# The third modulation vector's row sum behind the values' product, `v`'s weight split ahead of that vector's parts, and the fifth vector's last parts amid later work

## What is computed

```python
mod = (silu(c) @ ada_w + ada_b).reshape(bsz, 6, dm)          # six vectors of 1024: ada 0 to 5
shift_a, scale_a, gate_a, shift_f, scale_f, gate_f = mod     # ada 2 is gate_a, 3 is shift_f, 4 is scale_f
h = rms_norm(x, norm1_g) * (1.0 + scale_a) + shift_a
proj = h @ w_in                                              # columns u, v, o, i, f, p
y_m = mlstm_group(u, v, o, i, f, ...)                        # convolution, q, k, decayed scores, their sum with v
y_p = pool_group(p, w_pool, b_pool, pool_scale)
x = x + gate_a * (concat([y_m, y_p]) @ w_out)
h = rms_norm(x, norm2_g) * (1.0 + scale_f) + shift_f         # then routing and 32 experts, then the second block
```

## Time and profile before

| | |
|---|---|
| median of 3 runs | 2020.95 us (2019.82, 2020.95, 2025.08) |
| the profiled execution's own time | 2019.93 us |
| its span | 2018.2 us |
| busy: TensorE, VectorE, ScalarE, GpSimd | 1944.6, 1184.1, 965.7, 186.4 us |
| mean granted TensorE clock | 0.992 |

### The profile page before, as it was taken

One profiled execution on the slowest core, in us unless ns is written; L12 is line 12 of the kernel. 1 busy time (PEld: TensorE's weight loads), 2 busy tenths in 40 slices (PEclk: granted clock), 3 DMA queues, 4 the chain that ended last, 5 costly groups with the idle time before them and its releaser, 6 DMA issues.

```text
span 2018.2 us, 22881 instructions
## 1 busy us (share of the span) xinstructions
PE 1944.6 (96%) x8920; PEld 1562.1 (77%) x8920; DVE 1184.1 (59%) x1548; ACT 965.7 (48%) x1469; POOL 186.4 (9%) x250
## 2 busy tenths in 40 slices
PE   4989989999999999999999999999999999999998
PEld 3757758888878888758888888887777778888886
DVE  7766699998989999763543323325345453333323
ACT  3443258888878888744232223224455542222221
POOL 3110111122111110020000000000021100000000
PEclk8999999999999999999999999999999999999999
DMA  8465379999999999951322232222212133323201
GB/s 292 146 214 193 125 248 370 366 377 378 380 363 357 362 373 366 345 169 69 105 84 89 99 105 84 94 94 68 86 59 83 43 115 105 103 85 105 94 32 42
DMA packets 199976, 366.49 MB, mean 182 GB/s; under 512 B 13466, under 2 KB 83879, under 8 KB 199866
## 3 DMA queue, kind: packets, MB, share of 16 engines
q1 hardware_dynamic: 180960, 342.91, 48.4%
q10 hardware_dynamic: 8858, 11.46, 1.7%
q0 software_dynamic: 10048, 10.62, 1.5%
HBM read 365.05 MB, written 24.65 MB: 193 GB/s over the span
## 4 chain that ended last, share of the span: by engine, by line
PE 81%; DVE 7%; DMA 6%; ACT 3%; issue 2%; SPq 1%; POOL 0%; DVEq 0%; POOLq 0%; ACTq 0%
PE ps L263 79%; DMA raw<-in_w_expert_gate 4%; DVE wlo L210 3%; DMA raw<-in_w_in 1%; ACT whi L191 1%; PE ps L2012 1%; PE ps L2039 1%; SPq L919 1%; DMA raw<-in_ada_w 0%; ACT YB L2104 0%; PE ps L2667 0%; DVE XT1l L2095 0%; DVE XT0l L2095 0%; DVE acc L260 0%; ACT XN L703 0%
## 5 line engine op out<-in xcount | busy, mean ns | idle before, releaser
L210 DVE TENSOR_TENSOR wlo<-raw,whi 128x1024 fp32r<-128x1024 f32 (+1 forms) x576 | 674.1, 1215 | 296.7 <-ACT whi L191 294.4
L191 ACT ACTIVATE whi<-raw 128x1024 fp32r<-128x1024 f32 (+1 forms) x576 | 573.5, 1048 | 233.4 <-PE ps L263 196.4
L263 PE MATMUL ps<-hT5h,whi 128*128 128x512 f32 x352 | 137.0, 389 | 0.6 <-DVE hT5l L260 0.6
L263 PE MATMUL ps<-hT3h,whi 128*128 128x512 f32 x352 | 137.0, 389 | 0.6 <-DVE hT3l L260 0.6
L263 PE MATMUL ps<-hT3h,wlo 128*128 128x512 f32 x352 | 137.0, 389 | 0.0
L263 PE MATMUL ps<-hT3l,whi 128*128 128x512 f32 x352 | 137.0, 389 | 0.0
L263 PE MATMUL ps<-hT5h,wlo 128*128 128x512 f32 x352 | 137.0, 389 | 0.0
L263 PE MATMUL ps<-hT5l,whi 128*128 128x512 f32 x352 | 136.9, 389 | 0.0
L2530 DVE TENSOR_TENSOR tmpT<-tmpT,ps 128x512 f32<-128x512 f32 x44 | 30.1, 684 | 139.7 <-PE ps L263 139.7
L263 PE MATMUL ps<-whi,XT1h 128*128 128x512 f32 x256 | 102.8, 401 | 1.5 <-DVE XT1l L2095 1.5
L263 PE MATMUL ps<-whi,XT0h 128*128 128x512 f32 x256 | 102.9, 402 | 1.2 <-DVE XT0l L2095 1.1
(11 more groups left out here) (446 smaller groups left out, 4045.0 us busy)
## 6 DMA issues: line engine op xcount, KB each, us to landing
raw<-in_w_expert_gate SPq DMA_DIRECT2D x64, 1024.0 KB, 7.4
raw<-in_w_expert_up SPq DMA_DIRECT2D x64, 1024.0 KB, 8.1
raw<-in_w_expert_down SPq DMA_DIRECT2D x64, 1024.0 KB, 7.0
raw<-in_ffn_w_gu SPq DMA_DIRECT2D x44, 1024.0 KB, 5.1
raw<-in_ffn_w_down SPq DMA_DIRECT2D x20, 1024.0 KB, 5.0
raw<-in_ada_w SPq DMA_DIRECT2D x24, 512.0 KB, 5.4
raw<-in_w_in SPq DMA_DIRECT2D x8, 1024.0 KB, 6.0
raw<-in_a_w_in SPq DMA_DIRECT2D x8, 1024.0 KB, 10.7
```

Source lines behind the costliest of these rows:

```text
L191: e.activation(hi[:, c], raw[:, c], ACT.Copy).then_inc(self.S("w_hi"), 1)
L210: e.tensor_tensor(lo[:, c], raw[:, c], hi[:, c].bitcast(F32), ALU.subtract).then_inc(self.S("w_lo"), 1)
L263: return e.matmul(o, l, r, start=start, stop=stop, skip_group_check=True)
```

## The change

The same instructions are issued on every engine; their order differs.

- TensorE: `ada_row_pe(3)` stands behind `n_pe("v")` instead of ahead of it.
- ScalarE: `ada_row_act(3)` stands behind the copies of the values and the split of the pooling group instead of ahead of `skip`.
- VectorE: `W.low` of `v`'s first item ahead of parts 12 to 15, that of its second right behind them; then `pool_out(2)` and `(3)`, parts 16 and 17, `W.low` of `wo`'s first item, parts 18 and 19. Parts 20 to 23 move between `scaled`, `finish`, `W.low` and `mix_low`.
- SyncE: `wo`'s first two items are loaded ahead of parts 16 and 18 instead of 18 and 22.

```diff
@@ first_sync
-                W.load(e, {2: 6, 4: 7, 8: 8, 18: 9, 22: 10}.get(m, 0))
+                W.load(e, {2: 6, 4: 7, 8: 8, 16: 9, 18: 10}.get(m, 0))
@@ first_pe
             pool_pe(e, 3)
+            n_pe(e, W.index["v"], "v", hT1, 0, KC, None)
             ada_row_pe(e, 3)
-            n_pe(e, W.index["v"], "v", hT1, 0, KC, None)
             sums_pe(e, 0)
@@ first_act
             W.high(e, W.index["v"][1] + 1)
-            ada_row_act(e, 3)
             for h in range(4):
                 skip(h)
...
                 e.activation(hT1[0][:, 4 + gi, :], PT[:, gi, 16:528], ACT.Copy).then_inc(S("mix_hi"), 1)
+            ada_row_act(e, 3)
             W.high(e, W.index["wo"][1] + 1)
@@ first_vec
             pooled(3)
-            ada_parts(e, own, 12, 13)
-            ada_parts(e, own, 14, 15)
             W.low(e, W.index["v"][0] + 1)
-            ada_parts(e, own, 16, 17)
+            ada_parts(e, own, 12, 13, 14, 15)
+            W.low(e, W.index["v"][1] + 1)
             pool_out(2)
             pool_out(3)
+            ada_parts(e, own, 16, 17)
+            W.low(e, W.index["wo"][0] + 1)
             ada_parts(e, own, 18, 19)
-            W.low(e, W.index["v"][1] + 1)
-            ada_parts(e, own, 20, 21)
-            W.low(e, W.index["wo"][0] + 1)
-            ada_parts(e, own, 22, 23)
...
             scaled(1)
+            ada_parts(e, own, 20)
             finish(0)
             W.low(e, W.index["wo"][1] + 1)
+            ada_parts(e, own, 21)
             scaled(2)
             finish(1)
             mix_low(0, UC[0], 5)
+            ada_parts(e, own, 22)
             scaled(3)
             mix_low(1, UC[1], 6)
             finish(2)
             mix_low(2, UC[2], 7)
+            ada_parts(e, own, 23)
             finish(3)
```

## The result

The changed kernel takes 2011.18 us (median of 6 runs, 2008.71 to 2012.20), the kernel before 2020.38 (6 runs, 2017.86 to 2025.08): a ratio of 0.9957 [0.9948, 0.9967], 0.43% or about 9 us faster. The profiled execution took 2008.71 us with a span of 2007.0, 2.5 us under the median. The page reads like that of before: the chain is TensorE's still, 84% of it (before 81%).

What follows compares the result with a forecast made beforehand. TensorE bounds the kernel; its 6.08 us wait for VectorE's chain of loads is charged again through half clock. 2019.93 - 9.4 + 0.6 = 2011.1, set at 2011.5 us; range 2008 to 2018.

Steps and rivals of the forecast that it cites:

- the sum: Whole kernel: profiled 2019.93 us, less 9.4 gained by TensorE, plus 0.6 lost on VectorE, gives 2011.1 us.
- `n_pe("v")` first, then the row sum: TensorE after `pool_pe`: `v` product starts without a wait, row sum at full clock, `sums_pe(0)` 9.38 us earlier.
- the copy's wait: TensorE ahead of `sums_pe(0)`: waiting for the copy of `v`'s last bank, 1.08 us, would be covered by the row sum.
- The second half of `v`'s weight: VectorE's split `W.low(v1)` would be ready before TensorE asks at 156.66; cost nothing.
- the cover: Time by which `v`'s second split is ready before TensorE asks: 1.8 us; without it each microsecond of delay costs one.
- `ada_row_act(3)`: ScalarE: its two copies, behind those of `v` and `mix_hi`, end near 171.8 and cost nothing, with 0.5 us margin.
- Parts 20 to 23: VectorE amid `scaled` and `finish`: cost 0.6 us, TensorE's wait for `mix_low(1)` growing from 0.7 to 1.3 us.
- SyncE: `wo2`'s load goes out later, about 188.4, lands at 195.4 and is in time with a cover of 4.5 us.
- The rest shifts as a whole: Behind 217 every wait hangs on TensorE or VectorE, so everything later moves earlier together.
- The rival that nothing arrives at the end: Expert stage: if its start is set by something not moved, the gain is lost there; 2020 us, chance 0.10.
- The scatter: Times of whole runs: half of the 5 us between the runs before was allowed for in the range.

Runs made afterwards that it cites:

- Experiment 1: Kernel before with only TensorE's and ScalarE's moves, VectorE's and SyncE's order left as it was: 2018.96 us against 2019.95, ratio 0.9999.
- experiment 5: Changed kernel with ScalarE's `ada_row_act(3)` back at its old place ahead of `skip`: 2019.97 us against 2019.86 for the kernel before, ratio 0.9999.
- experiment 2: Kernel before with six matmuls of no use filling TensorE's wait ahead of the row sum: 2018.04 us against 2019.95, ratio 0.9992.
- Experiment 3: Changed kernel with the split of `v`'s second item behind `pool_out` and parts 16 and 17: 2017.53 us against 2019.95 for the kernel before.
- Experiment 8: Changed kernel with parts 20 and 21 and `mix_low(1)` earlier on VectorE: 2009.75 us against 2019.78 for the kernel before, ratio 0.9955.
- Experiment 6: Changed kernel with `wo0` and `wo1` loaded at their old places: 2017.04 us against 2019.86 for the kernel before, ratio 0.9986.
- experiment 4: Changed kernel with parts 20 to 23 right behind 18 and 19: 2020.19 us against 2019.95 for the kernel before, ratio 1.0004.
- second trace: The changed kernel run once more, unaltered: 2011.10 us against 2019.78 for the kernel before, ratio 0.9960.
- seventh: Changed kernel with three matmuls of no use in TensorE's pause ahead of the ranking: 2008.98 us against 2019.86 for the kernel before, ratio 0.9950.
- ninth: Changed kernel with parts 20, 21 and `mix_low(1)` earlier on VectorE, fillings ahead of ranking and first gathered rows: 2009.18 us, again 2008.47 us.

## Why the prediction was right

The forecast was 2011.5 us and 2011.18 was measured, by the mechanism of the sum: the marks show a gain of 9.10 us where the sum had 8.8. That the median came within 0.3 us of the forecast is in part luck. The interval of the ratio leaves a gain of 6.7 to 10.5 us, and the forecast took only about half of the 1.0 us between the profiled execution and the median, without saying why; the whole of it would have given 2012.1. By its steps:

- **`n_pe("v")` first, then the row sum.** Predicted 25.91 us from `pool_pe` to `sums_pe(0)` (143.70 to 169.61), measured 25.92. Both halves of `v` came in time, the clock held 1.00, the copy's wait vanished under the row sum. 35.29 - 25.92 = 9.37 against 9.38 predicted. Experiment 1 shows that it needs the split of `v` ahead of the parts, experiment 5 that it needs ScalarE's order too, and experiment 2 bounds the clock's part at 2 us.
- **The second half of `v`'s weight.** No cost, as predicted, but in the first trace the cover was 1.2 us and not 1.8 (157.80 against 156.6). I had taken 4.97 us, a single reading, from the end of part 13 to part 15 being ready; measured (146.04 + 2.60 = 148.64 to 154.16) it is 5.52. That is the scatter of the loads and not the megabyte, which I had rightly put at nothing: in the eight traces with the changed kernel's order and loads at this place the cover is 1.2 to 2.2 us, with 1.8 inside. So the forecast's figure is a middle one, and its weak point is that it stood without a spread. Experiment 3 shows what lay behind: a price of one for one, and the clock.
- **`ada_row_act(3)`.** Its copies, done by 172.9, held up nothing on TensorE.
- **Parts 20 to 23.** Predicted 0.6 us, measured 0.27 (9.37 at `sums_pe(0)`, 9.10 at the ranking). Mechanism and place were right: the wait for `mix_low(1)` grew from 0.73 us to 1.08 rather than 1.3, as VectorE was a little quicker than my sum. The second copies of `scaled(3)` start at 192.94 with part 22 right ahead of them, as the step said. Experiment 8 removes this wait.
- **SyncE.** `wo2`'s load was issued at 188.11, 187.0 on before's clock of marks (less 1.14), against the 188.4 that I had put, and ScalarE did not wait for it. Experiment 6 shows what I had left out: I priced the loads of `wo0` and `wo1` at their new places only, and did not ask what the change would be worth at the old ones. By the distance it would keep 5.5 of its 9.1 us; by the medians 2.8, with an interval of 0.8 to 5.0.
- **The rest shifts as a whole.** This held at the ranking (9.10) and in the medians (9.2). The rival that nothing arrives at the end is refuted: the expert stage took 567.3 and 567.6 us in the changed kernel's two traces, 569.7 before.
- **The scatter.** The 5 us between the runs before were taken into the range as unexplained. At most 1.7 us of such scatter is now explained, below.

## What to carry to other kernels

When an engine waits for a long chain of loads, look at what stands behind it in its queue: if the next work needs only something that another engine has ready but does later, move the two together on every engine that touches them, since one move alone only renames the wait. Count the cover of each step that moves, in microseconds, and read the new trace for that distance first; it tells a change of 0.3 us, where the run time of this kernel does not tell 3. Filling a wait so that the clock holds gives back less than the clock's cost wherever a second engine has been using the slow stretch to catch up.

## What the runs showed of the hardware

- **The same pause does not always halve the clock.** The pause of 3.2 us ahead of the ranking stands in all ten traces without filling there. The clock stayed at 1.00 behind it in the kernel before and in experiment 4, and the distance from the ranking to the first gathered rows was 12.61 and 12.66 us. It fell to 0.50 to 0.57 in the eight others: the distance was 13.08 to 13.32 us in five of them (the changed kernel's second trace, experiments 1, 3, 5 and 6) and 14.31 to 14.35 in three (its first trace, experiments 2 and 8), in which the slow stretch lasted about twice as long. With filling it was 12.68 to 12.73 in three traces. So the half clock cost 0.4 to 0.7 us or 1.7 us here. The Trainium skill, "TensorE: Matmul & The Clock Gate", What's actually happening, says that the activity is watched in a window that runs freely and does not start with the kernel, so that the slow stretch at a kernel's start differs from run to run. That these traces differ at a pause in the middle fits it; the cause was not tried apart.
- **This explains only a little of the scatter.** One-core times of one kernel lie 3 to 10 us apart, and those of the seventh and ninth kernels, with the clock held at the ranking, still 3.4 to 6.7 us. The join behind the experts (18.6 to 21.8 us) and the expert stage (566.1 to 571.4 us) scatter by more than the clock's 1.7 us, and why they do so was not tried.
- **Loads of 512 KB differ by about a microsecond from trace to trace.** With two in flight on SyncE's queue, the step from the end of part 13 to the addition of part 15 took 4.54 to 5.52 us in thirteen traces. A megabyte issued right behind on the same queue made no difference that stands out (4.54 to 5.52 us in nine traces with it, 4.85 to 5.27 in four without). Two traces alone, 2.71 against 2.15 us between two additions, would have said otherwise.
